# One layer-normalising product instead of two: a VectorE add ahead of it, and the product moved inside the next unit

## The reference, cut to what matters

```python
def rmsnorm(x, g):
    xf = x.astype(jnp.float32)
    y = xf * lax.rsqrt(jnp.mean(xf * xf, axis=-1, keepdims=True) + EPS)
    return (y * g.astype(jnp.float32)).astype(x.dtype)
...
    y = y + d_skip.astype(f32)[:, None] * xs
    y = y.reshape(bsz, seq, M2_WIDTH)
    y = rmsnorm(y * jax.nn.silu(z.astype(f32)), norm_g)
```

## Time and profile before

| | before |
|---|---|
| median of 3 runs | 1312.68 us (1311.46 to 1314.19) |
| the profiled execution's own time | 1313.04 us |
| its span, first to last instruction | 1311.3 us |
| TensorE busy | 1291.3 us (98%) |
| VectorE busy | 848.4 us (65%) |
| GpSimd busy | 636.7 us (49%) |
| ScalarE busy | 492.9 us (38%) |

### The profile page before, as it was taken

One profiled execution on the slowest core, in us unless ns is written; L12 is line 12 of the kernel. 1 busy time (PEld: TensorE's weight loads), 2 busy tenths in 40 slices (PEclk: granted clock), 3 DMA queues, 4 the chain that ended last, 5 costly groups with the idle time before them and its releaser, 6 DMA issues.

```text
span 1311.3 us, 15989 instructions
## 1 busy us (share of the span) xinstructions
PE 1291.3 (98%) x6218; PEld 1055.1 (80%) x6218; DVE 848.4 (65%) x1142; ACT 492.9 (38%) x758; POOL 636.7 (49%) x302
## 2 busy tenths in 40 slices
PE   7999999999999999999999999999999999999999
PEld 4888887788888888888878888867888888888887
DVE  7789894846888117775237798677477761377720
ACT  6333556744323112223334235566442221122220
POOL 2986662144444444443468775512444444444442
PEclk9999999999999999999999999999999999999999
DMA  6232321033333223333233223201333333233332
GB/s 216 79 104 66 89 88 42 25 97 113 96 96 115 91 85 96 97 96 111 83 97 96 82 66 97 87 25 53 94 111 97 96 106 104 80 97 97 108 111 86
DMA packets 40939, 120.49 MB, mean 92 GB/s; under 512 B 6432, under 2 KB 10656, under 8 KB 40864
## 3 DMA queue, kind: packets, MB, share of 16 engines
q1 hardware_dynamic: 40864, 119.46, 28.8%
HBM read 114.20 MB, written 2.10 MB: 89 GB/s over the span
## 4 chain that ended last, share of the span: by engine, by line
PE 90%; DVE 4%; ACT 2%; POOL 2%; DMA 1%; issue 0%; SPq 0%; POOLq 0%
PE bank L504 26%; PE bank L517 26%; PE bank L509 24%; PE bank L718 3%; PE bank L506 1%; ACT G L1077 1%; PE bank L766 1%; DMA raw<-in_w_in 1%; POOL wl L362 1%; PE bank L663 1%; PE bank L755 1%; DVE G L1566 1%; PE bank L596 1%; PE bank L611 1%; PE bank L620 1%; PE bank L745 1%
## 5 line engine op out<-in xcount | busy, mean ns | idle before, releaser
L362 POOL TENSOR_TENSOR wl<-raw,wh 128x1024 fp32r<-128x1024 f32 (+3 forms) x208 | 506.7, 2437 | 628.1 <-ACT wh L901 392.0
L901 ACT ACTIVATE wh<-raw 128x1024 fp32r<-128x1024 f32 (+3 forms) x208 | 218.6, 1052 | 266.0 <-PE bank L509 205.4
L504 PE MATMUL bank<-xl,wh 128*128 128x512 f32 x1088 | 281.7, 397 | 0.0
L517 PE MATMUL bank<-xh,wl 128*128 128x512 f32 x1088 | 272.4, 392 | 0.0
L509 PE MATMUL bank<-xh,wh 128*128 128x512 f32 x1056 | 260.9, 389 | 0.0
L504 PEld LDWEIGHTS bank<-xl,wh 128*128 128x128 f32 x1088 | 202.9, 188 | 47.1 <-issue 4.9
L517 PEld LDWEIGHTS bank<-xh,wl 128*128 128x128 f32 x1088 | 203.2, 188 | 43.0 <-issue 1.4
L509 PEld LDWEIGHTS bank<-xh,wh 128*128 128x128 f32 x1056 | 198.2, 188 | 41.5
L1228 DVE TENSOR_TENSOR x<-x,bank 128x512 f32<-128x512 f32 x64 | 43.8, 685 | 228.6 <-PE bank L517 228.6
L504 PE MATMUL bank<-ml,wh 128*128 128x512 f32 x512 | 137.5, 395 | 0.0
L517 PE MATMUL bank<-mh,wl 128*128 128x512 f32 x512 | 127.5, 389 | 0.0
(11 more groups left out here) (304 smaller groups left out, 1357.8 us busy)
## 6 DMA issues: line engine op xcount, KB each, us to landing
raw<-in_w_gu SPq DMA_DIRECT2D x88, 512.0 KB, 3.5
raw<-in_w_in SPq DMA_DIRECT2D x52, 512.0 KB, 3.6
raw<-in_w_dn SPq DMA_DIRECT2D x32, 704.0 KB, 4.1
raw<-in_w_ol SPq DMA_DIRECT2D x16, 384.0 KB, 3.0
raw<-in_w_oe SPq DMA_DIRECT2D x16, 256.0 KB, 2.6
x<-in_x SPq DMA_DIRECT2D x8, 256.0 KB, 6.4
raw<-in_w_first SPq DMA_DIRECT2D x4, 512.0 KB, 4.5
out_x<-x SPq DMA_DIRECT2D x8, 256.0 KB, 4.5
```

The lines of the kernel that those rows point to most:

```text
L362: tt(wl[:, p, 0:cols], raw[:, p, 0:cols], wh[:, p, 0:cols].bitcast(F32), ALU.subtract).then_inc(wl_full, 1)
L504: mm(bank[b][:, :], wh[:, p, k * P:(k + 1) * P], lo[:, k, :], start=(k == 0), stop=False)
L517: w = mm(bank[b][:, :], wl[:, p, k * P:(k + 1) * P], hi[:, k, :], start=False, stop=(k == K - 1))
L901: fn(wh[:, p, 0:cols], raw[:, p, 0:cols], ACT.Copy).then_inc(wh_full, 1)
```

## The change

VectorE adds the two tiles of squares, `xbc[:, 2] + xbc[:, 3]`, into `xbc[:, 2]`, and raises a new semaphore `m2sq_summed`. The add stands between `emit_low` and `s5_back` at s = 15, behind a wait for both squares. `m2_norm` then is one product of ones with the sum. It no longer stands behind unit 16 but inside unit 17, at a new hook `between`, which is called after the first pass (L504) and before the second (L509). Nothing else moves.

```diff
-            def unit(b, K, hi, lo, out, ready=None, within=None, each=None):
+            def unit(b, K, hi, lo, out, ready=None, within=None, each=None, between=None):
...
                         mm(bank[b][:, :], wh[:, p, k * P:(k + 1) * P], lo[:, k, :], start=(k == 0), stop=False)
...
+                    if between is not None:
+                        between()
                     if ready is None:
                         for k in ks:
                             w = mm(bank[b][:, :], wh[:, p, k * P:(k + 1) * P], hi[:, k, :], start=False, stop=False)
...
             def m2_norm():
                 claim(7, act_free[7])
-                for i in range(2):
-                    pe.wait_ge(m2sq_ready, nth(m2sq_ready))
-                    w = mm(bank[7][:, :], ones, xbc[:, 2 + i, :], start=(i == 0), stop=(i == 1))
-                w.then_inc(act_bank[7], 1)
+                pe.wait_ge(m2sq_summed, nth(m2sq_summed))
+                mm(bank[7][:, :], ones, xbc[:, 2, :], start=True, stop=True).then_inc(act_bank[7], 1)
...
                         unit(unit_bank(s), KD, xh, xl, xbc_silu if 2 <= s <= 7 else unit_out,
-                             within=lambda: beside(s - 1))
+                             within=lambda: beside(s - 1), between=m2_norm if s == 17 else None)
...
-                    if s == 16:
-                        m2_norm()
...
                     if 14 <= s <= 15:
                         emit_low(MIXB + s % 2, G[:, 4 + s % 2, :])
                     if s == 15:
+                        dve.wait_ge(m2sq_ready, 2 * (l + 1))
+                        tt(xbc[:, 2, :], xbc[:, 2, :], xbc[:, 3, :], ADD).then_inc(m2sq_summed, 1)
+                    if s == 15:
                         s5_back(l, 0)
```

More of the change, by code:

```diff
@@ L219, in build @@
             sem(n) for n in ("xbt_ready", "logs_ready", "m2_exp", "mix_ready", "mix_read")]
-        yz_ready, m2sq_ready, m2_rms = sem("yz_ready"), sem("m2sq_ready"), sem("m2_rms")
+        yz_ready, m2sq_ready, m2sq_summed, m2_rms = [sem(n) for n in ("yz_ready", "m2sq_ready", "m2sq_summed", "m2_rms")]
         tab_full, cf_ready, s5_scanned = sem("tab_full"), sem("cf_ready"), sem("s5_scanned")
```

## The result

The median went from 1312.28 us (6 runs) to 1318.51 us (6 runs, 1317.74 to 1318.81): ratio 1.0043, 95% interval 1.0032 to 1.0054. The change is slower, by 0.43%.

What follows compares the result with a forecast made beforehand. TensorE, busy 98%, was taken as the bound. Stalls for the add of +2.06 and +2.12 us, +4.2 together, took the profiled 1313.04 to 1317.2, the median to 1316.9 (+0.32%); range 1312.2 to 1318.6.

Steps and rivals of the forecast that it cites:

- What the change can give: TensorE around unit 17: one product for two, with the sum in time, gains 0.87 us a layer, 1.7 in all.
- the wait of 0.47 inside the old norm: TensorE's old norm: the second product's weights load 0.47 us late, because the second square ends at 134.62.
- When the sum is there: VectorE's add behind `emit_low`: stands for GpSimd's first L362 until 137.93, then runs until 138.48 in layer 1.
- the row at 190 us: Earlier meeting in the profile: GpSimd's L362 took the turn after `emit_low`; VectorE's L1544 stood, taking 2.90 us.
- Rival 1: VectorE's add gets the turn at once, ending at 136.24: -0.18 us a layer, 1312.3 in all; chance 0.14.
- Rival 3: VectorE's add stands behind both of GpSimd's L362: +4.4 us a layer, 1321.5 in all; chance 0.04.
- The sum: TensorE stands some 2.9 us for the add in unit 17: +2.06 us layer 1, +2.12 layer 2, together +4.2.
- the stated range: Range for the median, 1312.2 to 1318.6 us, meant to leave out no more than 2 in 10.
- the forecast's own: Narrower range from the spread of the runs, 1315.6 to 1318.4 us, holding about 7 in 10.
- What else moves: Around unit 17: `s5_back` some 2.9 us later, the norm's factor 3.9 later, at no cost; nothing gives the loss back.
- the 2 us to spare: L611, reader of `s5_back`'s L1441 on TensorE: comes 2 us after its input is ready, 2.7 before.
- the four signs that were to show the prediction wrong: Add's record about 0.7 us; add ending behind second L362; L611 waiting for L1441; unit 18 not 2.1 us late in layer 1.

Runs made afterwards that it cites:

- e8: Changed kernel with VectorE's order at s = 15 made add, `s5_back`, `emit_low`: 1311.07 us against 1312.78 for the kernel before, ratio 0.9989.
- e4: Changed kernel without the add, the two old products standing at the new place in unit 17: 1313.17 us against 1312.92 before, ratio 1.0001.
- e9: Changed kernel with the second square written to PSUM bank 7, so the add reads one PSUM operand: 1312.85 us against 1313.19 before, ratio 0.9996.
- e5: The changed kernel run once more, unaltered: 1319.49 us against 1312.78 for the kernel before, ratio 1.0050.
- e1: Changed kernel with VectorE's add ahead of `emit_low` instead of behind it: 1314.00 us against 1312.92 for the kernel before, ratio 1.0008.
- e3: Changed kernel with the single product later in unit 17, behind s5_out and s5_in, ahead of the third pass: 1324.14 us against 1312.92 before, ratio 1.0084.
- e7: Changed kernel with the change in layer 2 only, layer 1 as before: 1315.40 us against 1312.78 for the kernel before, ratio 1.0020.
- e2: Changed kernel with GpSimd's low part of unit 17's weights ahead of s5_imaginary: 1314.82 us against 1312.92 for the kernel before, ratio 1.0015.
- e10: Changed kernel with the add and single product, but the product kept behind unit 16: 1324.78 us against 1313.19 for the kernel before, ratio 1.0090.
- e6: Changed kernel with 12 extra matmuls ahead of the product's wait, their result overwritten: 1316.48 us against 1312.78 for the kernel before, ratio 1.0029.

## Why the prediction was right, point by point

**What the change can give.** One product in place of two was put at 0.87 us a layer; e8 measures 0.82 and 0.77 by the yardstick, 1.7 us by the runs. The bookkeeping behind it was a little off: the wait of 0.47 inside the old norm, from which I read only the lags, was not part of its price (e4); the second product was.

**When the sum is there.** The decisive step was who has the turn at the end of `emit_low`, and the row at 190 us answered it. The add's record is 2.83 us for about 2.9 predicted, GpSimd first, VectorE ahead of the second L362. Rival 1 put 1312.3 on the case that the add does not stand; e9, which makes it so, lies 0.34 under its own runs of before, for 0.4 predicted; that is within the noise of the runs, but the yardstick is 0.23 and 0.18 lower in the two layers. Rival 3 did not occur. By the Trainium skill, "SBUF — State Buffer", section "Who interferes with whom", only the port pair that VectorE and GpSimd share causes such contention, and it is an exclusive lock: this trace agrees, with 2.83 us for two SBUF operands and 0.68 for one.

**The sum.** This is the term that was mis-sized. The prediction priced a stall of 2.9 us at 2.06 and 2.12 us in the layers, +4.2 in all. Measured without a fall, it is 1.99 (layer 2) and in e5 1.92 (layer 1): right to 0.15. What it left out is the clock behind the stall: 8.76 against 7.32 in layer 1, 8.95 against 7.38 in layer 2, so 1.4 to 1.6 us more where it falls, which in either profile was one layer of two. With one fall the yardsticks add up to +5.35; the runs show +6.2, with an interval from 4.2 to 7.1. The median of 1318.51 lies 0.1 inside the upper end of the stated range, and 0.1 outside the forecast's own. That end was drawn for the spread of the runs and not for a fall, so that the number came out inside it is luck; e5's median, 6.7 above its own runs of before, would have been outside. I had read the clock at 1.00 in all slices as a property of the kernel; it holds for the kernel whose trace I read, and says nothing of one with a new stall. The Trainium skill, "TensorE: Matmul & The Clock Gate", section "HAM oscillation — how this bites in real kernels", says that waits between bursts of matmuls can throttle TensorE anew; the windows of after agree, with 0.50 behind the stall.

**What else moves.** L613 did not wait in the changed kernel, as predicted; the 2 us to spare were real, since in e1 and e3, where TensorE comes earlier, it stood 1.0 and 2.0 (weight loads). Nothing behind unit 17 gave the loss back. Of the four signs that were to show the prediction wrong, three stayed away and one came: unit 18 starts 3.5 us late in layer 1 (148.90 - 133.24 = 15.66 us behind unit 17's start, before 146.17 - 134.01 = 12.16), not 2.1. In layer 2, without a fall, it is 2.0.

## What to carry to other kernels

When work goes from a full engine to one with time left, look at the instant, not the share: VectorE was busy 65%, but at this place it stood behind GpSimd with instructions of two SBUF operands, and a 0.7 us add took 2.8. Put such an instruction where the other engine is between two instructions, give it a PSUM operand, or order the list so that the one which must stand has no reader near (e8). Price a stall of TensorE with the clock that it may cost behind it: here 1.9 to 2.0 us a layer without a fall and 3.4 to 3.6 with one.

## What the runs showed of the hardware that was not expected

- The granted clock fell to 0.50 behind stalls in the middle of dense work: behind one of the two stalls of 2.9 to 3.0 us in both profiles of the changed kernel, behind the one of 3.0 in e7, behind the second stall of 2.6 in both layers of e3, and at both stalls of 4.7 and 4.8 (e10). It did not fall behind the stalls of 2.1 in e2. Since it fell behind 2.6 and not behind 3.0, the length of the stall alone does not decide; what does was not tried.
- At the start of the program the windows show 1.00 throughout, but the matmuls behind the first wait of 8.6 us are as slow as at 0.50:

```profile
8.56 2.07 PE L532 MATMUL bank<-G,ones_first 128*128 128x512 f32 x2 [8.56 <-ACT wh L899]
```

  From 13.22 on the same pair takes 1.02, and e10's L689 at 0.50, of the same form, takes 2.05. So a granted clock of 1.00 in a window there does not say that the matmuls ran at the upper level.
- A float32 product of 128x512 with a 128x128 matrix costs TensorE about 0.87 us (e4: two in 1.75), where a matmul of the units' form starts every 0.23 (1.81 for 8).
- Filling both stalls with 12 useless matmuls each made the program 3.0 us faster (e6 against e5).
